# A two-layer diffusion step on one core: where the tiles of the modulation matrix are multiplied

## The reference

```
def _adaln(cond, w, b):
    return jax.nn.silu(cond) @ w + b
...
def _block(x, mod, s0, lp, ffn):
    shift1, scale1, gate1, shift2, scale2, gate2 = jnp.split(mod[:, None, :], N_MOD, axis=-1)
    m, s_fin = _mixer(x * (1 + scale1) + shift1, lp, s0)
    x = _layer_norm(DEEPNORM_ALPHA * x + gate1 * m, lp['ln_g'][0], lp['ln_b'][0])
    f = ffn(x * (1 + scale2) + shift2)
    x = _layer_norm(DEEPNORM_ALPHA * x + gate2 * f, lp['ln_g'][1], lp['ln_b'][1])
    return x, s_fin
...
for l in range(DEPTH):
    mod_ctx = _adaln(c_ctx[None], w_ada[l], b_ada[l])
    mod_lat = _adaln(c, w_ada[l], b_ada[l])
    xp, s_ctx = _block(xp, mod_ctx, s0_ctx, lp, ffn)
    xs, _ = _block(xs, mod_lat, state_wkv[:, l], lp, ffn)
```

## Time and profile before

| what | value |
|---|---|
| median of 3 runs | 2448.92 us |
| the three runs | 2445.35, 2448.92, 2464.73 us |
| span of the profiled execution | 2456.2 us |
| busy: PE, PEld, DVE, ACT, POOL | 88%, 75%, 46%, 33%, 5% |
| mean clock granted to TensorE | 0.908 |
| moved over the whole span | 301 MB, 123 GB/s |

### The profile page before, as it was taken

The page is one execution under the profiler, slowest core; times in us unless marked ns, Lnnn a source line. Parts: engine busy times, 40 slices in busy tenths (PEclk is TensorE's granted clock), DMA queues, the critical chain, the costliest instruction groups (busy, mean ns, idle before and its releaser), DMA issues. The chain is left out here.

```text
span 2456.2 us, 31677 instructions
## 1 busy us (share of the span) xinstructions
PE 2161.2 (88%) x13765; PEld 1846.5 (75%) x13765; DVE 1120.2 (46%) x1369; ACT 816.9 (33%) x957; POOL 114.9 (5%) x161
## 2 busy tenths in 40 slices
PE   7888999989677998878888886778999999999996
PEld 2386776766566997768777774668899899898895
DVE  0154443232556554633444435654455454454554
ACT  0143232333223443332323323224333343343343
POOL 2001100010002000010101100000000000000000
PEclk9997999999798999856789887979999999999998
DMA  9831232232315555310101012234555655555552
GB/s 293 270 110 35 87 104 87 87 104 88 120 35 164 178 188 176 112 34 18 35 27 45 20 51 69 69 103 138 192 168 172 197 174 181 183 168 191 176 169 89
DMA packets 247418, 301.31 MB, mean 123 GB/s; under 512 B 8427, under 2 KB 224080, under 8 KB 247152
## 3 DMA queue, kind: packets, MB, share of 16 engines
q1 hardware_dynamic: 240112, 286.28, 36.4%
q0 software_dynamic: 4192, 11.28, 1.5%
q10 hardware_dynamic: 2976, 1.73, 0.2%
HBM read 297.69 MB, written 1.57 MB: 122 GB/s over the span
## 5 line engine op out<-in xcount | busy, mean ns | idle before, releaser
L1326 DVE TENSOR_TENSOR WL<-WRING,WH 128x2048 fp32r<-128x2048 f32 (+1 forms) x237 | 516.2, 2179 | 565.7 <-ACT WH L1063 564.2
L639 PE MATMUL PS<-HTH,WH 128*128 128x256 f32 x2448 | 721.4, 295 | 39.1 <-issue 22.1
L641 PE MATMUL PS<-HTH,WL 128*128 128x256 f32 x2448 | 708.1, 289 | 0.0
L640 PE MATMUL PS<-HTL,WH 128*128 128x256 f32 x2448 | 708.0, 289 | 0.0
L1063 ACT ACTIVATE WH<-WRING 128x2048 fp32r<-128x2048 f32 (+1 forms) x237 | 431.4, 1820 | 697.9 <-PE PS L641 444.9
L639 PEld LDWEIGHTS PS<-HTH,WH 128*128 128x128 f32 x2448 | 482.0, 197 | 53.2 <-issue 42.6
L640 PEld LDWEIGHTS PS<-HTL,WH 128*128 128x128 f32 x2448 | 480.4, 196 | 0.2
L641 PEld LDWEIGHTS PS<-HTH,WL 128*128 128x128 f32 x2448 | 478.8, 196 | 0.0
L673 PE MATMUL PS<-WRING,CONDT 128*2 128x256 f32 x768 | 192.2, 389 | 6.3 <-DMA WRING<-in_w_ada 6.0
L952 PE MATMUL PS<-WH,AH 128*128 128x512 f32 x440 | 171.8, 391 | 13.0 <-DVE WL L1326 13.0
L1178 ACT ACTIVATE GM<-PS 128x512 fp32r<-128x512 f32 x112 | 66.7, 597 | 325.6 <-PE PS L804 325.4
(11 more groups left out here) (331 smaller groups left out, 2561.4 us busy)
## 6 DMA issues: line engine op xcount, KB each, us to landing
WRING<-in_exp_w_in SPq DMA_DIRECT2D x80, 1024.0 KB, 5.4
WRING<-in_w_ada SPq DMA_DIRECT2D x48, 1024.0 KB, 5.2
WRING<-in_w_in SPq DMA_DIRECT2D x42, 1024.0 KB, 5.4
WRING<-in_exp_w_out SPq DMA_DIRECT2D x40, 1024.0 KB, 4.9
WRING<-in_ffn_w_in SPq DMA_DIRECT2D x22, 1024.0 KB, 5.2
WRING<-in_ffn_w_out SPq DMA_DIRECT2D x11, 1024.0 KB, 4.9
WRING<-in_w_o SPq DMA_DIRECT2D x8, 1024.0 KB, 5.0
WRING<-in_exp_w_in SPq DMA_DIRECT2D x16, 512.0 KB, 3.9
```

The costliest lines, as they stand in the source:

```text
L639: mm(out, h[:, kb, c], hi[:, kb, :], start=kb == 0, stop=False)
L640: mm(out, h[:, kb, c], lo[:, kb, :], start=False, stop=False)
L641: last = mm(out, s[:, kb, c], hi[:, kb, :], start=False, stop=kb == k - 1)
L1326: tt(WL[:, m % 2, 0:k * w], WRING[:, n % RING, 0:k * w], WH[:, m % 2, 0:k * w].bitcast(F32), ALU.subtract)\
```

## The change

Only the first 8 `w_ada` tiles of layer 0 stay in the opening. The other 16 go to the scan's fill of layer 0, ahead of the first 8 tiles of layer 1; these too make 24. The last 16 tiles of layer 1 go to the fill of layer 1's own scan, which had none. The number of `w_ada` tiles, their matmuls and their loads stay what they were.

```diff
 ADA = 6 * D // 256
+ADA_HEAD = 2 * D // 256
...
     sched = [("cond",)]
-    for j in range(ADA):
+    for j in range(ADA_HEAD):
         sched.append(("ada", 0, j, 0, 2))
         sched += [("turn", 0, j - 1), ("col", 0, j - 1)] if j else [("bias",)]
         sched += [("ada", 0, j, 1, 2), ("row", 0, j)]
-    sched += [("turn", 0, ADA - 1), ("col", 0, ADA - 1), ("consts",), ("params", 0), ("barrier",)]
+    sched += [("turn", 0, ADA_HEAD - 1), ("col", 0, ADA_HEAD - 1), ("consts",), ("params", 0), ("barrier",)]
...
         fill, pieces = [], 8 if l + 1 < LAYERS else 4
+        behind = [(l, j) for j in range(ADA_HEAD, ADA)] + [(l + 1, j) for j in range(ADA_HEAD) if l + 1 < LAYERS]
         for i in range(8, FILL_TO):
             fill += [(("part", l, i, p, pieces), []) for p in range(pieces)]
             fill[-1] = (fill[-1][0], [(1, ("later", l, i))])
-            for j in range(ADA * (i - 8) // (FILL_TO - 8), ADA * (i - 7) // (FILL_TO - 8) if l + 1 < LAYERS else 0):
-                fill += [(("ada", l + 1, j, p, 4), []) for p in range(4)]
-                fill[-1] = (fill[-1][0], [(1, ("row", l + 1, j)), (2, ("turn", l + 1, j)), (3, ("col", l + 1, j))])
+            for m, j in behind[len(behind) * (i - 8) // (FILL_TO - 8):len(behind) * (i - 7) // (FILL_TO - 8)]:
+                fill += [(("ada", m, j, p, 4), []) for p in range(4)]
+                fill[-1] = (fill[-1][0], [(1, ("row", m, j)), (2, ("turn", m, j)), (3, ("col", m, j))])
```

## The result

The change made the kernel faster by less than 1%: the median of eleven runs is 2436.77 us (2430.73 to 2440.36) against 2448.92 us (2439.56 to 2465.74), and the ratio of the runs is 0.9931 (95% interval 0.9902 to 0.996). The forecast was 2400 us. The time lies outside its range of 2378 to 2426 us and beside rival (b), 2440 us. The profiled execution has a span of 2428.9 us, 27.3 us under the span of before.

What follows compares the result with a forecast made beforehand. The prediction took PE to bound the opening, with transfers close, and the lower clock to weigh on layer 1's scan. Span 2456.2 - 60.1 + 11 = 2407 us; median 2448.9 - 49 = 2400 us, range 2378 to 2426.

Steps and rivals of the forecast that it cites:

- rival (b): Layer 1's scan: the clock does not recover and the pieces cost their full price; 2440 us, chance 0.12.
- The opening: Before the first product: sixteen tile periods of 3.76 us go, -60.1 us, with no load taking their place.
- Layer 0's scan: Its fill keeps 24 `w_ada` tiles at the same places with the same shapes; price nothing, scan of 413 us.
- layer 1's scan: It takes in 16 tiles: +51.2 us at the full clock, -40 us by the clock, net +11 us, to 408 us.
- Step 2: Layer 1's scan: a tile costs 3.2 us at the full clock, from the difference between the two layers' scans.
- 85%: Scan fill: a tile's price of 3.2 us as a share of the 3.76 us it takes alone.
- The 0.45: Layer 1's scan: cost in us of each us at the lower clock, from stretches between chain starts.
- Step 3: Layer 1's scan: 16 added tiles cut time at the lower clock from 175 to 86 us, recovering 40 us.
- (a): Layer 1's scan: the clock recovers wholly, no more time at the lower level than layer 0's; 2380 us, chance 0.20.
- (c): Layer 1's scan stays at clock 0.78, a tile costs over 3.76 us (5.4); slower, 2475 us, chance 0.04.

Runs made afterwards that it cites:

- b_l0solo: Kernel before, with the 24 `w_ada` tiles of layer 0's fill standing alone ahead of that scan; median 2516.7 us, ratio 1.026 to the kernel before.
- b_pieces8_cut: Kernel before, with layer 1's `w_in` tiles in 8 pieces and the split apart from the mix; median 2429.4 us, ratio 0.9922 to the kernel before.
- x_quarter: Changed kernel, with only 2 of the 8 matmuls of each of layer 1's last 16 `w_ada` tiles; median 2440.0 us, ratio 0.9982 to the kernel before.
- x_double: Changed kernel, with each matmul of layer 1's last 16 `w_ada` tiles done twice; median 2455.7 us, ratio 1.0039 to the kernel before.
- x_pairs: Changed kernel, with two `w_ada` tiles behind each of layer 1's first eight `w_in` tiles, none behind the last three; median 2401.0 us, ratio 0.9749 to before.
- x_cut: Changed kernel, with layer 1's split an item of its own, two pieces behind the mix; median 2424.0 us, ratio 0.984 to the kernel before.
- x_pieces8: Changed kernel, with layer 1's `w_in` tiles cut into 8 pieces, as layer 0's are; median 2417.2 us, ratio 0.980 to the kernel before.
- x_ten: Changed kernel, with layer 1's 16 `w_ada` tiles over the first ten `w_in` tiles, none behind the last; median 2428.0 us, ratio 0.9893 to before.
- x_late: Changed kernel, with two `w_ada` tiles behind each of layer 1's last eight `w_in` tiles, none behind the first three; median 2423.6 us, ratio 0.9917 to before.
- before_again: Kernel before, unchanged, profiled once more; median 2447.1 us, ratio 1.0004 to the kernel before.
- b_cut: Kernel before, with layer 1's split an item of its own, two pieces behind the mix; median 2451.9 us, ratio 1.0023 to the kernel before.

## Why the prediction was wrong

**The opening (-60.1 us): right**, -57.9. No load took its place. **Layer 0's scan (0): right**, to 0.1 us, where a repeat of either kernel is 3 us longer. **The direction, and that layer 1's scan decides: right.** The term that failed is layer 1's, +11 us where the profiles have +32.2. It was made of two numbers, and both were too good.

**Step 2, the price of a tile, failed first.** It took 3.2 us a tile from the difference between two scans. With a us at the lower level at its measured half, the changed kernel paid 375 - 309 = 66 us, 4.1 a tile. Of the 15 us that were missing, the runs place about 9 in the price itself: within layer 0's scan b_l0solo gives 3.75 us. A part of these 9 is the clock price, since the prediction's difference gives 3.4 us when a us at the lower level is taken at one half; the rest is the base, layer 1's scan with its coarser pieces and its blocks, for against b_pieces8_cut the same difference gives 3.7. The prediction also let the one half act on the recovery only; it raises the price of a tile with it (to 3.3 by its six stretches), so that its sum would have fallen by some 2 us and not by 4.

That 3.75 equals the 3.76 of the opening doesn't show that a scan hides nothing: it is what is left after 19 us of waits for `XS` have gone, and alone a tile took 3.59 us in one place and 4.05 in another. What is shown is that matmuls are paid in full or nearly so at the margin (at full 43 us for 43 in x_quarter, 49 for 58 in x_double), and that the "85%" was too low. The 0.45 itself came from unlike stretches, of which the two long ones held 12 matmuls more than three of the four short ones; the same kernel profiled twice gives 0.49 to 0.56. The Trainium skill's one half, in the term list of "TensorE: Matmul & The Clock Gate", agrees with these better than the rows of single stretches did.

The other 5 or 6 us are the place and the length of the pieces: I said that the pieces stood between the steps of the same chains as in layer 0, but six of layer 1's eleven gaps hold a single tile, and its `w_in` pieces are twice as long. x_pairs gets 5 us of it back at full, x_cut 7, x_pieces8 6. Which of the two, place or length, counts for how much isn't separated.

**Step 3, the clock, failed by less, and is the larger lesson.** I took the time at the lower level to fall in proportion to the number of tiles, from 177 to 86 us; it fell to 110, 34 us of recovery at one half against the 40 forecast. That it falls with PE's work is shown: a quarter of the matmuls leaves 207, once 110, twice 58. That the number of tiles is not its measure is shown too: the same 16 tiles leave 58, 92, 96 or 110 us, by where they stand (x_pairs, x_ten, x_late, the change). With x_pairs the forecast's total would have come out, 2401 us against 2400, but with a scan of 398 us and not 408, by a clock that recovered more than foreseen beside a price that was higher, which is luck and no support for the steps. Why the same work in another order leaves 38 us more at the lower level (x_late against x_pairs) is open: neither the waits for `XS` nor one end of the scan accounts for it.

**The base was an execution from the long side.** The span was 2456.2 us, and I moved the whole gain to the median. In before_again the same scan is 15.0 us shorter; against that profile the change costs 47 us in layer 1's scan and brings 16 us in all, which is near what the runs show (0.7% of 2449 is 17 us; the medians differ by 12).

**The rivals.** (b), 2440 us, is where the time came out, but not by its way: the clock did recover by 67 us, and the price was higher. (a) was reached by no kernel: the fewest us at the lower level in layer 1's scan are 58, against 45 in layer 0's. The point that (c) names was passed: at 4.1 us a tile costs more at the full clock than the 3.76 it saves in the opening (66 us against 58), and what keeps the change from being slower is the clock alone.

## What to carry to other kernels

A price taken as the difference between two stretches holds every other thing in which they differ; measure it within one stretch, by taking the work out of the fill there. Where filler work also holds the clock up, its net cost is the small difference of two large terms (66 and 34 us here), so look for the placement before counting tiles, and profile the kernel before twice. And an engine that gets two helpers' work in one block makes the dependent chain wait for both: keep such blocks apart by at least one step of the chain (worth 7 us at the full clock in x_cut, and no gain in the runs of b_cut).

## What the runs showed of the hardware

Leaving out 96 fp32 matmuls, 43 us of PE's work, made nothing faster (x_quarter), since the granted clock of the scan fell from 0.87 to 0.76. The same 16 tiles, with the same matmuls, leave 58, 92, 96 or 110 us at the lower level, by their places between the steps. Float32 matmuls with a weight of only two columns hold the clock: it was 1.00 over 75 us of the opening in which PE did hardly anything else. The Trainium skill, in Part 1 of "TensorE: Matmul & The Clock Gate", has it that activity releases the throttle; the three amounts of matmuls (207, 110 and 58 us at the lower level) agree. And the granted clock of one program is not the same in each execution: 177 and 150 us at the lower level in one scan of the kernel before, 110 and 116 in the changed one.
